# Modulation folds, embedding split, shift products and final normalization reordered in a one-core transformer kernel

## Chip, cores and metric

The kernel runs on 1 core of one Trainium2 chip. The metric is the device time of one execution in microseconds, the median of several runs. The input is one sequence of 512 tokens with 1024 features in float32.

## What is computed

The reference applies three layers to x (512 x 1024). All of it is float32.

```python
# block 1: attention heads beside a short convolution
h = rms_norm(x, pre_norm_gain); q, k, v, z_a, b, c, u, z_c = split(h @ w_in, 8)
attn = rms_norm(diff_attention(q, k, v, lam, slopes), subln_gain) * 0.8 * silu(z_a)   # 4 heads
conv_out = b * causal_conv3(c * u) * silu(z_c)
x = x + rms_norm(concat(attn, conv_out) @ w_out, post_norm_gain)
x = x + sigmoid(x @ w_ple_gate) * rms_norm(p @ w_ple_proj, ple_norm_gain)   # p: embedding, 256 wide
# two modulated layers, i = 0 (Fourier mixer), i = 1 (retention mixer)
sh1, sc1, g1, sh2, sc2, g2 = split(silu(c) @ w_ada[i] + b_ada[i], 6)
x = x + g1 * mixer(rmsnorm(x, g) * (1 + sc1) + sh1)
x = x + g2 * swiglu(rmsnorm(x, g) * (1 + sc2) + sh2)
# end
shf, scf = split(silu(c) @ w_ada_final + b_ada_final, 2)
return rmsnorm(x, final_norm_g) * (1 + scf) + shf
```

The modulation is 14 vectors of 1024 numbers, each the product of one vector of 1024 with a 1024 x 1024 matrix.

## The kernel before

**Layout and the main loop.** Activations lie feature-major, eight slices of 128 features by 512 tokens. Every large product runs in three passes: weights and activations are each split in a high part (float32r) and the rest, and TensorE adds lo x hi, hi x lo and hi x hi in PSUM (`mul`, lines 1708, 1711, 1712; the same for halves of the tokens in lines 1724 to 1728). Weights come as a stream of chunks of 128 x 1024 (eight 128 x 128 tiles) through a ring of four slots: SyncE's queue loads a chunk (line 336), ScalarE writes its high part (`split_w`, line 443), GpSimd writes the rest in four quarters (`lo_part`, line 411), TensorE uses it. TensorE needs 24 matmuls of 512 columns for a chunk. Each engine executes its own written list in order, and semaphores tie the lists together.

**Modulation.** A matrix of the modulation comes as eight chunks of 128 x 1024, loaded by the same SyncE queue between weight chunks (line 342, a ring of two slots; a load waits until the step that used the slot is done). VectorE adds each chunk, times its column of c, to `ada_acc` (one *step*: line 945 for the first of eight, line 948 for the others). The 128 partial sums of each of the 1024 results then have to be added over the partitions. In the four attention heads this is `ada_turn`: TensorE transposes the eight blocks of `ada_acc` into two PSUM banks (line 1895), VectorE adds each along its columns (line 965) and adds the bias (line 967). In the later layers it is `ada_fold` and `ada_rows`: VectorE transposes 32 x 32 blocks (line 972) and adds (line 973), TensorE finishes with four small products (line 1886).

**Attention heads.** A loop over the heads. Inside, TensorE's list holds tiles 4 to 7 of this head with the scores and transposes of the attention between them, and then tiles 8 to 11, the first four of the next head (queries, keys, values, gate). Between them `body_tail` puts, after the n-th product, the weighted values (n = 2), the norm's sum (n = 9) and the modulation's transposes (n = 17). After tile 10 TensorE waits until VectorE has scaled the next head's queries and keys out of PSUM (`evacuate`, line 1208), and computes their first scores (line 1991). VectorE's loop begins with these two evacuations, and ends with the split of the attention's output (line 1285) and `ada_out`. After the last head the projection `out` takes the place of tiles 8 to 11.

**Embedding.** After the heads ScalarE's queue loads the embedding p, ScalarE waits for it and splits it (line 621), VectorE subtracts (line 1296); only then come the weight splits and modulation steps of the projection. The embedding is used by the product after the projection.

**Fourier layer.** `dft1` turns features: four groups g, four token tiles tt each. `rinv_columns` (line 2040) adds the squares for the norm and stands after (g, tt) = (2, 2); ScalarE and VectorE read dft1's tiles with that norm (lines 722, 1381). `shift_columns` (lines 2051, 2052), the products of the shift with the same table, stand after the last tile. `dft2` turns tokens, VectorE combines halves (lines 1410 to 1423) and splits (line 1398), then comes the product `fout`. Modulation steps 41 to 48 stand here: one after group 1, one each in groups 2 and 3, five ahead of the residuals.

**End.** The last normalization works on the front and the back 256 tokens. VectorE computes X x gain x root for each of eight slices (`scaled`, line 1663), ScalarE adds the shift to it (`finish`, line 906; the last two slices on VectorE, line 1680), and the result is stored.

Of the kernel before, what the change touches and what calls it, by code (L numbers as in the profile page):

```python
# [138 lines left out]
def build(nc, W, ADA, XT, PT, COLS, DIST, ROPE, DECAY, OUT):  # L139
# [3 lines left out]
    with ctx:  # L143
# [3 lines left out]
        def sem(name):  # L147
            return ctx.enter_context(nc.semaphore(name))
# [59 lines left out]
        lamt = scr[:, 15 * S:15 * S + 256]  # L208
        MIX, E = area(0, 8), area(8, 8)
# [27 lines left out]
        ada_sum, ada_folded = sem("ada_sum"), sem("ada_folded")  # L237
# [195 lines left out]
        def _(act):  # L433
# [186 lines left out]
            act.wait_ge(p_in, 16)  # L620
            act.activation(b_hi[:, 8:10, :].rearrange("p k s -> p (k s)"), PV, ACT.Copy).then_inc(p_hi, 1)
            c0, t0 = CH["out"], TI["out"]
            for n in range(8):
                if n != 3:
                    split_w(flat, c0 + n + 4)
                if n >= 3:
# [91 lines left out]
            for z in range(2 * NH):  # L718
                wait_tile(act, flat, t1 + z)
                for h in range(2):  # L720
                    half, tt = slice(2 * P * h, 2 * P * (h + 1)), 2 * (z % 2) + h
                    ins = act.activation(a_hi[:, z, half], banks[:, BANK[t1 + z], half], ACT.Identity, bias=zero,
                                         scale=rcol[:, tt:tt + 1])
                ins.then_inc(z_hi, 1)
                if z == 3:
                    act.wait_ge(aux_ready, AUX["fshift"] + 1)
                    split_w(flat, c0 + 4, free=True)
# [176 lines left out]
            def finish(m, scaled, part, done):  # L904
                act.wait_ge(scaled, m + 1)
                act.activation(X[:, m, part], X[:, m, part], ACT.Identity, bias=vector(12)(m)).then_inc(done, 1)
# [18 lines left out]
        def _(dve):  # L925
# [26 lines left out]
            def ada_out(u, g, at=flat, bank=None):  # L952
# [7 lines left out]
                if bank is None:  # L960
                    dve.tensor_tensor(dst, aux[:, 0:KD], b, ALU.add).then_inc(aux_free, 1)
                    return
                for n, half in enumerate((bank, 7)):
                    turned = banks[:, half, :].rearrange("p (f q) -> p f q", q=P)
                    ins = dve.tensor_reduce(ada_col[:, 4 * n:4 * n + 4], turned, AX.X, ALU.add)
                link(ins, at)
                dve.tensor_tensor(dst, ada_col, b, ALU.add).then_inc(aux_free, 1)

            def ada_fold(g, at=flat):
# [4 lines left out]
                                  ALU.add).then_inc(ada_folded, 1)  # L974

# [184 lines left out]
            link(dve.memset(G[:, 0:2], 0.0))  # L1160
            dve.wait_ge(r_ready, 1)
# [55 lines left out]
            with dve.Fori(0, NH) as i:  # L1217
# [70 lines left out]
                ada_out(A0 + 6, 0, at, 4)  # L1288
# [6 lines left out]
            dve.wait_ge(p_hi, 1)  # L1295
            dve.tensor_tensor(b_lo[:, 8:10, :].rearrange("p k s -> p (k s)"), PV,
                              b_hi[:, 8:10, :].rearrange("p k s -> p (k s)").bitcast(fp32),
                              ALU.subtract).then_inc(p_ready, 1)
            t0 = TI["out"]
            for n in range(8):  # L1300
# [5 lines left out]
                ada(k=(1, 1, 1, 1, 1, 2, 1, 0)[n])  # L1306

# [82 lines left out]
            dve.wait_ge(aux_free, AUX["fshift"] + 1)  # L1390
            t0 = TI["dft2"]
# [38 lines left out]
            ada(k=5)  # L1430
# [231 lines left out]
            def scaled(m, part, done):  # L1662
                dve.scalar_tensor_tensor(out=X[:, m, part], in0=X[:, m, part], scalar=gs[:, m:m + 1],
                                         in1=rinv[:, part], op0=ALU.mult, op1=ALU.mult).then_inc(done, 1)
# [5 lines left out]
            scaled(0, FRONT, half_scaled)  # L1670
            scaled(1, FRONT, half_scaled)
            back_tile_made(7, t0, KD - 1, 11)
            for m in range(2, KD):
                scaled(m, FRONT, half_scaled)
            dve.wait_ge(r_ready, 8)
            for m in range(KD):
                scaled(m, BACK, x_scaled)
            dve.wait_ge(x_scaled, KD)
            for m in range(KD - 2, KD):
                dve.tensor_scalar(X[:, m, BACK], X[:, m, BACK], vector(12)(m), None, ALU.add).then_inc(fin, 1)  # L1680
# [3 lines left out]
        def _(pe):  # L1684
# [274 lines left out]
            def body_tail(at, n):  # L1959
# [6 lines left out]
                if n == 17:  # L1966
                    ada_turn(at, A0 + 6, 0, 4)
# [87 lines left out]
            for g in range(NH):  # L2055
                pe.wait_ge(xl, 2 * g + 2)
                for tt in range(TB):
# [330 lines left out]
```

## Time and profile before

| | us |
| --- | --- |
| median of 3 runs | 1554.79 |
| lowest, highest | 1554.63, 1555.78 |
| profiled execution, its own time | 1554.12 |
| its span in the profile | 1552.0 |
| TensorE matmuls, busy | 1537.0 (99%) |
| VectorE, ScalarE, GpSimd busy | 790.5, 597.4, 869.6 |
| last matmul begins | 1542.26 |

The span runs from the first to the last recorded event; the execution's own time is 2.1 us longer. TensorE's matmuls are pipelined: one of 512 columns is shown with 0.39 us, and the next begins 0.23 us after it. So its list is best read by the distance between beginnings, not by the busy share. Times of day below are microseconds from the start of the span.

### The profile page before, as it was taken

What the parts mean: (1) busy time and instruction counts of PE and PEld (TensorE: products, weight loads), DVE (VectorE), ACT (ScalarE), POOL (GpSimd) and SP (SyncE); (2) the same over time, 40 slices, a digit from 0 to 9 for tenths busy, and PEclk for the clock granted to TensorE, in tenths of its full rate; (3) what the DMA queues carried; (4) which work ended last, traced back from release to release, by engine and by line L of the source; (5) the groups of instructions that cost most, each with busy time, mean ns of one, the idle gap of its engine ahead of it and who ended that gap; (6) DMA issues with size and microseconds to landing.
All of it is one profiled execution on the core that took longest, in us unless ns stands there. A gap on an engine that the chain in (4) does not pass through costs nothing.

```text
span 1552.0 us, 21277 instructions
## 1 busy us (share of the span) xinstructions
PE 1537.0 (99%) x7254; PEld 1273.8 (82%) x7254; DVE 790.5 (51%) x1128; ACT 597.4 (38%) x885; POOL 869.6 (56%) x1040
## 2 busy tenths in 40 slices
PE   9999999999999999999999999999999999999997
PEld 7777878887988888888888888888889888888886
DVE  6887776878645543551545424446257454011113
ACT  7444434685522212223444334244345322122223
POOL 6445538647567765775463635535535766555551
PEclk9999999999999999999999999999999999999999
DMA  6534455226265555542232322313212563223321
GB/s 231 191 128 155 164 214 189 82 84 205 95 216 176 202 198 183 192 160 95 89 114 67 109 82 80 97 52 106 95 54 82 201 206 120 98 95 95 95 82 55
DMA packets 58249, 202.97 MB, mean 131 GB/s; under 512 B 6480, under 2 KB 8528, under 8 KB 58192
## 3 DMA queue, kind: packets, MB, share of 16 engines
q1 hardware_dynamic: 56752, 198.74, 37.6%
q10 hardware_dynamic: 1440, 3.44, 0.7%
q8 instruction: 40, 0.66, 0.2%
q14 instruction: 17, 0.14, 0.0%
HBM read 200.05 MB, written 2.10 MB: 130 GB/s over the span
## 4 chain that ended last, share of the span: by engine, by line
PE 76%; POOL 12%; issue 11%; DVE 0%; DMA 0%; ACT 0%; SPq 0%; POOLq 0%; DVEq 0%; ACTq 0%
PE banks L1708 20%; PE banks L1712 20%; PE banks L1711 20%; POOL w_lo L411 12%; PE banks L2212 2%; PE banks L2211 2%; PE banks L2208 2%; PE banks L1724 1%; PE banks L1727 1%; PE banks L1728 1%; PE banks L2248 1%; PE banks L2247 1%; PE banks L2246 1%; PE banks L2235 0%; PE banks L2234 0%
## 5 line engine op out<-in xcount | busy, mean ns | idle before, releaser
L411 POOL TENSOR_TENSOR w_lo<-w_raw,w_hi 128x256 fp32r<-128x256 f32 x1028 | 862.6, 872 | 646.9 <-ACT w_hi L443 646.9
L443 ACT ACTIVATE w_hi<-w_raw 128x1024 fp32r<-128x1024 f32 x257 | 270.1, 1057 | 640.7 <-PE banks L1708 576.0
L1708 PE MATMUL banks<-a_hi,w_lo 128*128 128x512 f32 x1228 | 483.4, 394 | 0.2 <-POOL w_lo L411 0.2
L1712 PE MATMUL banks<-a_hi,w_hi 128*128 128x512 f32 x1228 | 478.2, 389 | 0.0
L1711 PE MATMUL banks<-a_lo,w_hi 128*128 128x512 f32 x1228 | 478.0, 389 | 0.0
L1708 PEld LDWEIGHTS banks<-a_hi,w_lo 128*128 128x128 f32 x1228 | 230.8, 188 | 49.0 <-issue 1.6
L1712 PEld LDWEIGHTS banks<-a_hi,w_hi 128*128 128x128 f32 x1228 | 230.5, 188 | 48.3
L1711 PEld LDWEIGHTS banks<-a_lo,w_hi 128*128 128x128 f32 x1228 | 230.6, 188 | 47.6 <-issue 1.0
L1708 PE MATMUL banks<-b_hi,w_lo 128*128 128x512 f32 x572 | 224.2, 392 | 2.3 <-POOL w_lo L411 2.1
L1712 PE MATMUL banks<-b_hi,w_hi 128*128 128x512 f32 x572 | 222.6, 389 | 0.0
L1711 PE MATMUL banks<-b_lo,w_hi 128*128 128x512 f32 x572 | 222.6, 389 | 0.0
L948 DVE SCALAR_TENSOR_TENSOR ada_acc<-ada_raw,small,ada_acc 128x1024 f32<-128x1024 f32 x98 | 149.5, 1525 | 47.5 <-DMA ada_raw<-in_ADA 45.5
L1105 DVE SCALAR_TENSOR_TENSOR X<-banks,mod,X 128x512 f32<-128x512 f32 x64 | 46.9, 749 | 164.1 <-PE banks L1712 163.9
L1708 PEld LDWEIGHTS banks<-b_hi,w_lo 128*128 128x128 f32 x572 | 107.4, 188 | 26.6 <-issue 3.8
L1711 PEld LDWEIGHTS banks<-b_lo,w_hi 128*128 128x128 f32 x572 | 107.4, 188 | 22.6 <-issue 0.5
L1712 PEld LDWEIGHTS banks<-b_hi,w_hi 128*128 128x128 f32 x572 | 107.3, 188 | 22.4
L1451 DVE TENSOR_TENSOR scr<-scr,banks 128x512 f32<-128x512 f32 x44 | 30.3, 688 | 112.3 <-PE banks L1712 111.9
L1447 DVE SCALAR_TENSOR_TENSOR scr<-scr,banks 128x512 f32<-128x512 f32 x44 | 30.2, 687 | 106.6 <-ACT scr L773 106.6
L1459 DVE SCALAR_TENSOR_TENSOR b_lo<-scr,b_hi 128x512 f32 (+1 forms) x44 | 33.2, 755 | 51.2 <-ACT b_hi L780 51.2
L2208 PE MATMUL banks<-w_lo,a_hi 128*128 128x512 f32 x128 | 49.8, 389 | 0.0
L2211 PE MATMUL banks<-w_hi,a_lo 128*128 128x512 f32 x128 | 49.8, 389 | 0.0
L2212 PE MATMUL banks<-w_hi,a_hi 128*128 128x512 f32 x128 | 49.8, 389 | 0.0
(287 smaller groups left out, 1632.7 us busy)
## 6 DMA issues: line engine op xcount, KB each, us to landing
w_raw<-in_W SPq DMA_DIRECT2D x258, 512.0 KB, 3.5
ada_raw<-in_ADA SPq DMA_DIRECT2D x112, 512.0 KB, 4.3
X<-in_XT SPq DMA_DIRECT2D x8, 256.0 KB, 6.4
scr<-in_DECAY ACTq DMA_DIRECT2D x4, 448.0 KB, 4.0
out<-X SPq DMA_DIRECT2D x2, 512.0 KB, 3.0
w_raw<-in_W SPq DMA_DIRECT2D x2, 256.0 KB, 3.8
scr<-in_PT ACTq DMA_DIRECT2D x1, 512.0 KB, 4.8
scr<-in_ROPE ACTq DMA_DIRECT2D x1, 512.0 KB, 4.6
```

Source lines behind the costliest of these rows:

```text
L411: pool.tensor_tensor(w_lo[:, c % RING, part], w_raw[:, c % RING, part], w_hi[:, c % RING, part].bitcast(fp32), ALU.subtract).then_inc(wlo, 1)
L443: act.activation(w_hi[:, c % RING, :], w_raw[:, c % RING, :], ACT.Copy).then_inc(whi, 1)
L948: ins = dve.scalar_tensor_tensor(out=ada_acc[:, :], in0=src, scalar=cact[:, f:f + 1], in1=ada_acc[:, :], op0=ALU.mult, op1=ALU.add)
L1105: ins = dve.scalar_tensor_tensor(out=X[:, m, :], in0=banks[:, BANK[t], :], scalar=mod[:, KD * g + m:KD * g + m + 1], in1=X[:, m, :], op0=A ...
L1451: read_out(dve.tensor_tensor(HD[:, n, :], SG[:, n, :], banks[:, BANK[u], :], ALU.mult), u)
L1459: dve.scalar_tensor_tensor(out=lo, in0=HD[:, n, :], scalar=0.5, in1=hi.bitcast(fp32), op0=ALU.mult, op1=ALU.subtract).then_inc(hid_ready, 1)
L1708: mm = pe.matmul(out, lo, x_hi, start=first, stop=False)
L1711: pe.matmul(out, hi, x_lo, start=False, stop=False)
L1712: mm = pe.matmul(out, hi, x_hi, start=False, stop=last)
L2208: mm = pe.matmul(out, a_hi[:, k, c], wl, start=(k == 0), stop=False)
L2211: pe.matmul(out, a_lo[:, k, c], wh, start=False, stop=False)
L2212: mm = pe.matmul(out, a_hi[:, k, c], wh, start=False, stop=(k == KD - 1))
```

## The change

Four edits, which share no instruction.

1. **Heads.** `ada_turn` is replaced by `head_ada_fold` on VectorE, ahead of `ada_out`, and `head_ada_rows` on TensorE, after n = 23, the last product of tile 10. Three small additions ahead of the loop make the matrix `head_fold`.
2. **Embedding.** ScalarE's wait and split, and VectorE's subtraction, stand after the third step of the projection's loop.
3. **Fourier.** `rinv_columns` stands one token tile later, `shift_columns` two token tiles earlier, ahead of dft1's last tile. ScalarE then waits for dft1's last tile in its place. Two modulation steps move from the five ahead of the residuals to the end of dft1.
4. **End.** VectorE multiplies X by the root alone, two slices at once; ScalarE applies the gain beside the shift.

```diff
             act.dma_start(PV, PT).then_inc(p_in, 16)
-            act.wait_ge(p_in, 16)
-            act.activation(b_hi[:, 8:10, :]..., PV, ACT.Copy).then_inc(p_hi, 1)
             for n in range(8):
                 if n != 3:
                     split_w(flat, c0 + n + 4)
+                if n == 2:
+                    act.wait_ge(p_in, 16)
+                    act.activation(b_hi[:, 8:10, :]..., PV, ACT.Copy).then_inc(p_hi, 1)
...
                 if z == 3:
-                    act.wait_ge(aux_ready, AUX["fshift"] + 1)
+                    wait_tile(act, flat, t1 + 2 * NH - 1)
                     split_w(flat, c0 + 4, free=True)
...
-            def finish(m, scaled, part, done):
-                act.wait_ge(scaled, m + 1)
-                act.activation(X[:, m, part], X[:, m, part], ACT.Identity, bias=vector(12)(m)).then_inc(done, 1)
+            def finish(m, rooted, part, done):
+                act.wait_ge(rooted, m // 2 + 1)
+                act.activation(X[:, m, part], X[:, m, part], ACT.Identity, bias=vector(12)(m),
+                               scale=gs[:, m:m + 1]).then_inc(done, 1)
...
+            def head_ada_fold(at):
+                dve.wait_ge(ada_sum, at("ada", KD))
+                dve.wait_ge(mix_ready, at("two", 2))
+                link(dve.transpose(head_turned, ada_acc[:, :]), at)
+                ins = dve.tensor_reduce(head_part, head_turned.rearrange("p (j q) -> p j q", q=32), AX.X, ALU.add)
+                ins.then_inc(head_folded, 1)
...
-                ada_out(A0 + 6, 0, at, 4)
+                head_ada_fold(at)
+                ada_out(A0 + 6, 0, at)
...
             dve.wait_ge(aux_free, AUX["fshift"] + 1)
+            ada(k=2)
             t0 = TI["dft2"]
...
             t0 = TI["fout"]
-            ada(k=5)
+            ada(k=3)
...
-            def scaled(m, part, done):
-                dve.scalar_tensor_tensor(out=X[:, m, part], in0=X[:, m, part], scalar=gs[:, m:m + 1],
-                                         in1=rinv[:, part], op0=ALU.mult, op1=ALU.mult).then_inc(done, 1)
+            def rooted(n, part, done):
+                x = X[:, 2 * n:2 * n + 2, part]
+                root = rinv[:, part].unsqueeze(1).broadcast_to([P, 2, HT])
+                dve.tensor_tensor(x, x, root, ALU.mult).then_inc(done, 1)
...
-            def ada_turn(at, u, g, bank):
-                pe.wait_ge(ada_sum, at("ada", KD * (g + 1)))
+            def head_ada_rows(at, u):
+                pe.wait_ge(head_folded, at("one", 1))
                 pe.wait_ge(aux_free, at("aux", u))
-                for f in range(KD):
-                    out = banks[:, bank if f < KD // 2 else 7, f % 4 * P:(f % 4 + 1) * P]
-                    mm = pe.transpose(out, ada_acc[:, f * P:(f + 1) * P], ident)
+                for b in range(4):
+                    mm = pe.matmul(aux[32 * b:32 * b + 32, 0:KD], head_fold, head_part[:, b:32:4], start=True, stop=True)
                 mm.then_inc(aux_ready, 1)
...
-                if n == 17:
-                    ada_turn(at, A0 + 6, 0, 4)
+                if n == 23:
+                    head_ada_rows(at, A0 + 6)
...
-                    if g == 2 and tt == 2:
-                        rinv_columns()
-            shift_columns().then_inc(aux_ready, 1)
+                    if g == 3 and tt == 1:
+                        shift_columns().then_inc(aux_ready, 1)
+                if g == 2:
+                    rinv_columns()
```

TensorE's list at the end of tile 10, in the heads' loop, before (line 1991: the next head's first scores; line 1895, the transposes, stands 18 matmuls further up):

```order
L1708 MATMUL banks<-a_hi,w_lo 128x512
L1711 MATMUL banks<-a_lo,w_hi 128x512
L1712 MATMUL banks<-a_hi,w_hi 128x512
L325 REGISTER_ALU
L1991 MATMUL banks<-scr 128x128 x2
L1697 REGISTER_ALU
L1708 MATMUL banks<-a_hi,w_lo 128x512
```

And now (line 1906: the four small products; lines 1720 to 1724 are `mul`, line 2002 the scores):

```order
L1720 MATMUL banks<-a_hi,w_lo 128x512
L1723 MATMUL banks<-a_lo,w_hi 128x512
L1724 MATMUL banks<-a_hi,w_hi 128x512
L1904 REGISTER_ALU
L1906 MATMUL banks<-scr 32x8 x4
L327 REGISTER_ALU
L2002 MATMUL banks<-scr 128x128 x2
```

Nothing stands between the modulation's product and the scores any more.

VectorE's list at the end of the same loop, before:

```order
L1285 TENSOR_TENSOR b_lo<-tmp,b_hi 128x512
L954 REGISTER_ALU
L965 TENSOR_REDUCE small<-banks 128x4 x2
L932 REGISTER_ALU
L967 ISA
L967 TENSOR_TENSOR mod<-small,cols 128x8
L1217 REGISTER_ALU
L1217 COMPARE_AND_BRANCH
```

And now:

```order
L1293 TENSOR_TENSOR b_lo<-tmp,b_hi 128x512
L977 STREAM_TRANSPOSE tmp<-ada_acc 128x1024
L936 REGISTER_ALU
L978 TENSOR_REDUCE scr<-tmp 128x32
L958 REGISTER_ALU
L964 ISA
L964 TENSOR_TENSOR mod<-banks,cols 128x8
L1225 REGISTER_ALU
L1225 COMPARE_AND_BRANCH
```

The branch leads back to the evacuations of queries and keys. Line 964 (`ada_out`) reads what TensorE's line 1906 writes, and it stands ahead of them.

VectorE's last instructions, before:

```order
L1663 SCALAR_TENSOR_TENSOR X<-X,gs,rinv 128x256 x2
L995 SCALAR_TENSOR_TENSOR X<-banks,mod,X 128x256
L1663 SCALAR_TENSOR_TENSOR X<-X,gs,rinv 128x256 x14
L1680 TENSOR_SCALAR X<-X,mod 128x256 x2
```

And now:

```order
L1676 TENSOR_TENSOR X<-X,rinv 128x2x256
L1000 SCALAR_TENSOR_TENSOR X<-banks,mod,X 128x256
L1676 TENSOR_TENSOR X<-X,rinv 128x2x256 x7
L1691 TENSOR_SCALAR X<-X,gs,mod 128x256 x2
```

Sixteen products of one slice became eight of two.

## Rows read from the trace of the kernel before

**Rows 1.** The page's part 1: busy time, share and instructions

```profile
PE 1537.0 (99%) x7254; PEld 1273.8 (82%) x7254; DVE 790.5 (51%) x1128; ACT 597.4 (38%) x885; POOL 869.6 (56%) x1040
```

**Rows 2.** Timeline, TensorE, first head's end: start, duration, engine, line, operation

```profile
71.21 0.39 PE L1712 MATMUL banks<-a_hi,w_hi 128*128 128x512 f32 x1
71.44 1.03 PE L1895 MATMUL banks<-cols,ada_acc 128*128 128x128 f32 x8
...
72.54 0.40 PE L1711 MATMUL banks<-a_lo,w_hi 128*128 128x512 f32 x1
...
76.18 0.39 PE L1712 MATMUL banks<-a_hi,w_hi 128*128 128x512 f32 x1
76.50 0.49 PE L1991 MATMUL banks<-scr 64*128 64x128 f32 x4
```

**Rows 3.** Timeline, VectorE, the same place

```profile
72.13 0.69 DVE L1285 TENSOR_TENSOR b_lo<-tmp,b_hi 128x512 f32 x1 [0.93 <-ACT b_hi L615]
...
74.19 0.17 DVE L967 TENSOR_TENSOR mod<-small,cols 128x8 f32 x1 [0.17 <-DVE small L965]
74.72 1.29 DVE L1208 TENSOR_TENSOR scr<-banks,scr 128x512 f32<-128x512 f32 x2 [0.37 <-issue]
```

**Rows 4.** Lines 972 and 973 by source: durations in ns, smallest, median, largest

```profile
L972 DVE STREAM_TRANSPOSE scr<-ada_acc x9: 1231/1246/1247, 423.1 to 1295.6; 128x1024 f32<-128x1024 f32 x9
L973 DVE TENSOR_REDUCE cols<-scr x9: 1221/1221/1223, 424.4 to 1296.9; 128x32 f32<-128x1024 f32 x9
```

**Rows 5.** Timeline, TensorE, the first later use of the small products

```profile
432.23 0.39 PE L1712 MATMUL banks<-a_hi,w_hi 128*128 128x512 f32 x1
432.55 0.25 PE L1886 MATMUL banks<-cols 128*32 128x8 f32 x8
...
433.07 0.39 PE L1711 MATMUL banks<-a_lo,w_hi 128*128 128x512 f32 x1
```

**Rows 6.** Timelines, ScalarE and TensorE, after the last head

```profile
233.83 1.06 ACT L621 ACTIVATE b_hi<-scr 128x1024 fp32r<-128x1024 f32 x1 [4.37 <-DMA scr<-in_PT]
...
239.30 0.39 PE L1712 MATMUL banks<-b_hi,w_hi 128*128 128x512 f32 x1
240.42 0.47 PE L1708 MATMUL banks<-b_hi,w_lo 128*128 128x512 f32 x1 [0.73 <-POOL w_lo L411]
```

**Rows 7.** Timelines, Fourier layer: TensorE, VectorE, SyncE's queue, ScalarE, GpSimd

```profile
333.45 0.39 PE L2068 MATMUL banks<-w_lo,b_hi 128*128 128x256 f32 x1 [0.36 <-DVE a_lo L1381]
...
353.34 0.74 DVE L945 TENSOR_SCALAR ada_acc<-ada_raw,small 128x1024 f32<-128x1024 f32 x1
...
355.71 1.27 DVE L948 SCALAR_TENSOR_TENSOR ada_acc<-ada_raw,small,ada_acc 128x1024 f32<-128x1024 f32 x1
...
363.22 1.75 DVE L948 SCALAR_TENSOR_TENSOR ada_acc<-ada_raw,small,ada_acc 128x1024 f32<-128x1024 f32 x1
...
354.11 0.33 SPq L342 DMA_DIRECT2D ada_raw<-in_ADA  x1
...
361.47 1.04 ACT L443 ACTIVATE w_hi<-w_raw 128x1024 fp32r<-128x1024 f32 x1
...
336.78 2.83 POOL L411 TENSOR_TENSOR w_lo<-w_raw,w_hi 128x256 fp32r<-128x256 f32 x4 [3.63 <-ACT w_hi L443]
...
362.59 9.82 POOL L411 TENSOR_TENSOR w_lo<-w_raw,w_hi 128x256 fp32r<-128x256 f32 x9 [1.71 <-ACT w_hi L443]
...
368.07 0.47 PE L1708 MATMUL banks<-b_hi,w_lo 128*128 128x512 f32 x1 [1.33 <-POOL w_lo L411]
```

**Rows 8.** Groups of ScalarE by line and shape: busy us, mean ns

```profile
L843 ACT ACTIVATE b_hi<-scr,small 128x512 fp32r<-128x512 f32 x16 | 11.0, 713 | 0.0
L682 ACT ACTIVATE b_hi<-X,small,gs 128x512 fp32r<-128x512 f32 x8 | 6.4, 802 | 0.0
```

**Rows 9.** Timelines, VectorE and ScalarE, the end

```profile
1541.67 5.62 DVE L1663 SCALAR_TENSOR_TENSOR X<-X,gs,rinv 128x256 f32<-128x256 f32 x14
...
1543.83 4.08 ACT L906 ACTIVATE X<-X,mod 128x256 f32<-128x256 f32 x10
```

More of the change, by code:

```diff
@@ L208, in build @@
         lamt = scr[:, 15 * S:15 * S + 256]
+        head_turned = tmp[:, :, :].rearrange("p a s -> p (a s)")
+        head_fold, head_part = scr[:, 14 * S + 64:14 * S + 96], scr[:, 14 * S + 96:14 * S + 128]
         MIX, E = area(0, 8), area(8, 8)
@@ L236, in build @@
         ada_in = [sem(f"ada_in{s}") for s in range(ADA_RING)]
-        ada_sum, ada_folded = sem("ada_sum"), sem("ada_folded")
+        ada_sum, ada_folded, head_folded = sem("ada_sum"), sem("ada_folded"), sem("head_folded")
         x_in = [sem(f"x_in{m}") for m in range(KD)]
@@ L619, in _ @@
             act.dma_start(PV, PT).then_inc(p_in, 16)
-            act.wait_ge(p_in, 16)
-            act.activation(b_hi[:, 8:10, :].rearrange("p k s -> p (k s)"), PV, ACT.Copy).then_inc(p_hi, 1)
             c0, t0 = CH["out"], TI["out"]
@@ L625, in _ @@
                     split_w(flat, c0 + n + 4)
+                if n == 2:
+                    act.wait_ge(p_in, 16)
+                    act.activation(b_hi[:, 8:10, :].rearrange("p k s -> p (k s)"), PV, ACT.Copy).then_inc(p_hi, 1)
                 if n >= 3:
@@ L950, in ada, with ada_out @@
                     ins.then_inc(ada_sum, 1)
-            def ada_out(u, g, at=flat, bank=None):
+            def ada_out(u, g, at=flat):
                 dve.wait_ge(aux_ready, at("aux", u + 1))
@@ L959, in ada_out @@
                     b = cols[:, bass.ds(at("eight", COL["b_ada"] + KD * g), KD)]
[L960 to L967, printed above, removed]
+                dve.tensor_tensor(dst, aux[:, 0:KD], b, ALU.add).then_inc(aux_free, 1)
             def ada_fold(g, at=flat):
@@ L1160, in _ @@
             link(dve.memset(G[:, 0:2], 0.0))
+            link(dve.tensor_tensor(head_fold, ident[:, 0:32], ident[:, 32:64], ALU.add))
+            for n in (2, 3):
+                link(dve.tensor_tensor(head_fold, head_fold, ident[:, 32 * n:32 * n + 32], ALU.add))
             dve.wait_ge(r_ready, 1)
@@ L1292, in _ @@
             steps[0] = 8 * NH
[L1295 to L1298, printed above, removed]
             t0 = TI["out"]
@@ L1306, in _ @@
                 ada(k=(1, 1, 1, 1, 1, 2, 1, 0)[n])
+                if n == 2:
+                    dve.wait_ge(p_hi, 1)
+                    dve.tensor_tensor(b_lo[:, 8:10, :].rearrange("p k s -> p (k s)"), PV,
+                                      b_hi[:, 8:10, :].rearrange("p k s -> p (k s)").bitcast(fp32),
+                                      ALU.subtract).then_inc(p_ready, 1)
             t1 = TI["ple"]
@@ L1669, in _ @@
                 wait_read(dve, flat, t0 + m)
-            scaled(0, FRONT, half_scaled)
-            scaled(1, FRONT, half_scaled)
+            rooted(0, FRONT, half_scaled)
             back_tile_made(7, t0, KD - 1, 11)
-            for m in range(2, KD):
-                scaled(m, FRONT, half_scaled)
+            for n in range(1, KD // 2):
+                rooted(n, FRONT, half_scaled)
             dve.wait_ge(r_ready, 8)
-            for m in range(KD):
-                scaled(m, BACK, x_scaled)
-            dve.wait_ge(x_scaled, KD)
+            for n in range(KD // 2):
+                rooted(n, BACK, x_scaled)
+            dve.wait_ge(x_scaled, KD // 2)
             for m in range(KD - 2, KD):
-                dve.tensor_scalar(X[:, m, BACK], X[:, m, BACK], vector(12)(m), None, ALU.add).then_inc(fin, 1)
+                dve.tensor_scalar(X[:, m, BACK], X[:, m, BACK], gs[:, m:m + 1], vector(12)(m), ALU.mult,
+                                  ALU.add).then_inc(fin, 1)
         @block.tensor
```

## The prediction, made before the changed kernel was run

> **What bounds the kernel.** I read the page's part 1 first: TensorE is busy 99% of the span, the others about half [rows 1]. That share overstates, since the matmuls are pipelined, so I then read TensorE's timeline by the distance between beginnings. A 512-column matmul begins 0.23 us after the one before (71.21 to 71.44 in [rows 2]), and nearly all of the list runs at that pace. A change can therefore gain only from work taken off TensorE's list, from the few waits in it, or from the end after the last matmul; and any wait added to the list is paid in full. The waits that the edits touch are 0.73 us after the last head [rows 6], 0.36 us ahead of dft1's last tile and 1.33 us in the product fout [rows 7]. The end is carried by VectorE and ScalarE together: 14 products in 5.62 us and 10 additions in 4.08 us, then a store [rows 9]. Anything else that VectorE or ScalarE does matters only where TensorE waits for it.
>
> **Edit 1, the heads.** *Removed from TensorE:* the transposes. The last product before them begins at 71.21, the second matmul after them at 72.54; without them that distance would be two paces, 0.46. They cost 1.33 - 0.46 = 0.87 us per head [rows 2]. *Added:* four small products. The same piece in the later layers takes 432.23 to 433.07 where 0.46 would do, so 0.38 us [rows 5]. Were that all, each head would gain 0.49.
>
> But the products now stand directly ahead of the next head's scores, and VectorE has two evacuations between them. I follow both engines through the first head's end, in the old trace's times.
> - TensorE: without transposes tile 10's last matmul begins at 76.18 - 0.87 = 75.31. The small products begin 0.32 later, as at 432.55 after 432.23 [rows 5]: 75.63.
> - VectorE: line 1285 ends at 72.82 [rows 3]. The block transpose, 1.246 us, needs its buffer and so starts when it has ended, about 72.87; the sum, 1.221 us, follows about 0.04 later [rows 4]. It ends at 75.38, 0.25 before TensorE asks. Tight, but no wait.
> - The small products end at 75.63 + 0.25 = 75.88 [rows 5]. VectorE's `ada_out` starts about 0.07 later, 75.95. From the start of `ada_out` to the end of both evacuations the old trace has 74.19 to 74.72 + 1.29 = 76.01, so 1.82 us, the loop's branch among it [rows 3]. They end at 77.77.
> - The scores can start at about 77.85. They started at 76.50 [rows 2].
>
> So each of the three heads that have a successor is 1.35 us *longer*: TensorE stands about 1.5 us between two pieces 0.25 and 0.49 us long, where before the evacuations were done 0.4 us before it asked. Three times 1.35 is +4.05. After the last head nothing waits for `ada_out`, and the 0.49 is gained: heads **+3.56**. Behind the wait on VectorE are the bias and the next softmax; they come 0.3 later relative to TensorE, whose next need of them is a tile (5 us) away: nothing. The two sums out of PSUM (line 965) go, 2.5 us of transpose and sum come; all of that is in the chain above. The three additions for `head_fold` run on VectorE before the heads' loop, where it waits for the first norm: nothing.
>
> **Edit 2, the embedding.** ScalarE stood 4.37 us for the load and 1.06 us in the split before its weight splits [rows 6], and TensorE paid for it once: 239.30 to 240.42 where 0.23 would do, 0.89 us. Moved behind three splits, the load has long landed, and two chunks go to GpSimd over 4 us sooner. If that cover failed, the most that could be lost is the old 0.89 again. VectorE's 1.2 us subtraction moves ahead of the first reads of the projection's tiles; seven banks let these be late. On SyncE's queue the chunk loads, which wait for GpSimd, and the modulation loads, which wait for steps, both come earlier. **-0.89.**
>
> **Edit 3, Fourier.** The norm's sums come one token tile later, filling a wait there, and so their readers on ScalarE and VectorE come about 0.3 later; the last dft1 tile waits for them [rows 7]. The shift products, about 0.5 us, now run inside that wait instead of after it. Net -0.2, which the next point absorbs. The two early steps fall in a stretch in which VectorE only waits for dft2's edge sums (its next step in [rows 7] is that of 353.34): nothing on VectorE. What they change is SyncE's queue. The load of step 43's chunk goes out at 354.11, after the first step ended (353.34 + 0.74), and every later weight chunk is queued behind it [rows 7]. Now it goes out some 10 us sooner. The wait of 1.33 us at 368.07 hangs on GpSimd's four quarters of fout's fourth chunk: ScalarE splits it at 361.47, GpSimd begins at 362.59 and TensorE goes on at 368.07, 5.4 us for four quarters that took 2.83 at 336.78, with VectorE's step of 1.75 us at 363.22 on top of it [rows 7]. The load of the step after group 3 was there early; now that load (step 46's) is queued behind a weight chunk that waits for GpSimd, goes out at about 361.2 and lands, with the chunk beside it, near 366. So GpSimd gets 363.7 to 366.4 to itself. Against it: the step after group 1 is now an addition to `ada_acc` (1.27) and not the first of eight (0.74, both in [rows 7]), which puts the later groups, the third chunk and ScalarE's split back by 0.4. I take TensorE's resumption at 367.0 instead of 368.07. The bounds are +0.4 (the delay adds, no relief) and -1.5 (wait and restart both gone). **-1.07.** The rule of the Trainium skill, SBUF — State Buffer, section "Who interferes with whom", is that a VectorE instruction with two SBUF inputs and a GpSimd instruction that reads SBUF exclude each other for a whole instruction. These rows show a slowing of 2.6 us beside VectorE's instructions and agree with it in kind. By the rule a step that landed before 366 would put a whole 1.27 us back, and this term would be near zero.
>
> **Edit 4, the end.** VectorE: a pair takes as long as a 128x512 product, 0.60 from start to start (two in 1.29, [rows 3]) instead of 2 x 0.40 (14 in 5.62, [rows 9]). ScalarE: the activation now reads a gain beside the shift. Lines with the one take 713 ns, with both 802 ns [rows 8]: +0.089, over twelve of them on this path. Ten additions in 4.08 begin 0.40 apart, and now 0.49: nine distances and the last one's own length give 9 x 0.1 + 0.09 = +0.98. Ahead of these ten stand four more with the same 0.09, and they wait for pairs, which come 0.14 to 0.2 later than single slices; part of it disappears in the wait for the last slice's square, so I count +0.40 for their start. They end at 1543.83 + 4.08 = 1547.91 before [rows 9], and at about 1549.3 now. VectorE's last two, of 14 products and two additions of about 0.3, ended near 1547.9 too; relieved, it ends near 1547.7 and no longer counts. The last store is issued when both are done, now by ScalarE. **+1.38.** The bounds are -0.7 (ScalarE's gain operand costs nothing in a back-to-back row and VectorE's relief shows) and +1.6.
>
> **Sum:** +3.56 - 0.89 - 1.07 + 1.38 = +2.98 us. The profiled execution took 1554.12 and would take 1557.1; the median of the runs is 0.67 above it, so I forecast **1557.8**. A measurement of this kernel can tell 0.2%, 3.1 us, from no change; the forecast lies just inside.
>
> **Rivals.**
> - *Relief fails (1559.3).* VectorE's fold ends after TensorE asks (only 0.25 us of room, and GpSimd works beside it), 0.2 us more in each of three heads, and the fourth chunk is not relieved (-1.07 becomes 0): 2.98 + 0.6 + 1.07 = +4.6. For it: the thin room, and the page's rule. Against: the fold's rows vary by under 20 ns.
> - *The round trip is partly hidden (1555.6).* If the wake-ups and the branch cost less than I count, a head is 0.6 longer, not 1.35: 2.98 - 2.2 = +0.8. Against: only fixed delays of rows are in the chain.
> - *Faster (1550.2).* The other side, in one mechanism: TensorE does not wait for the evacuations, because VectorE gets past `ada_out` before tile 10 ends. Then every head gains 0.49: -1.96 in place of +3.56. With fout's wait fully gone (-1.5) and the end at its lower bound (-0.7) that is about -5, 1549.7; with the other terms as forecast 1552.3. It decides at 76.4 us: the evacuations must end before TensorE's scores could start. In VectorE's list they stand behind a wait for the very product that follows tile 10, so I see little room.
> - *The end costs nothing (1556.4).* Both engines share the end; if the gain operand is free, +1.38 becomes 0.
>
> **How the numbers follow.** Forecast 0.55, split evenly by the 0.2% bound because it lies on it (0.27 slower, 0.28 same); relief fails 0.20, slower; partly hidden 0.13 and end free 0.05, same; faster 0.07. That is faster 0.07, same 0.46, slower 0.47. The range takes in the first four cases with their bounds: 1554.6 to 1559.8.
>
> **What would show it.** In the changed profile: scores (now line 2002) starting about 1.9 us after the small products, with VectorE's evacuations ended just before, three times; the distance from head to head 1.35 us longer; no wait at the projection's second half; the fourth fout chunk's wait under 0.5 us; line 909 at about 0.58 us each and ten of them in 5 us; the last store issued 1.4 us later behind the last matmul. A head shorter than before would make the prediction wrong at its root.

## The result, and the profile after

The changed kernel takes 1561.69 us (median of 6 runs, 1558.71 to 1562.65), the one before 1555.04 in 6 runs beside it (1554.63 to 1557.02). The ratio is 1.0035, with a 95% interval of 1.0024 to 1.0045. So it is slower, as forecast, but by 6.65 us between the medians and not by 3, and the time is above the range of 1554.6 to 1559.8. The means of the same runs lie 5.6 us apart, nearer to the ratio: two of the six runs were near 1559. The profiled execution took 1561.93, with a span of 1559.9 instead of 1552.0.

The page's part 1 of the changed kernel, which answers to [rows 1]:

```profile
PE 1538.0 (99%) x7254; PEld 1273.4 (82%) x7254; DVE 800.3 (51%) x1123; ACT 598.4 (38%) x885; POOL 864.7 (55%) x1040
```

TensorE has as many instructions as before and its busy time has risen by 1.0 us; the share says nothing. What tells is the start of the same TensorE instruction in both traces:

| place on TensorE | before | after | difference |
|---|---|---|---|
| first scores of head 1 | 27.58 | 27.97 | +0.39 |
| scores of head 2 | 76.50 | 79.32 | +2.82 |
| scores of head 3 | 129.06 | 134.99 | +5.93 |
| scores of head 4 | 181.62 | 190.58 | +8.96 |
| start of the first dft1 tile, past the last head and the embedding | 320.27 | 327.72 | +7.45 |
| product fout, third chunk | 361.02 | 368.77 | +7.75 |
| product fout, fourth chunk | 368.07 | 374.85 | +6.78 |
| statistics products after the last matmul of the model | 1541.07 | 1548.23 | +7.16 |
| span | 1552.0 | 1559.9 | +7.9 |

The heads cost 2.4, 3.1 and 3.0 us, and I had forecast 1.35 each. The windows view shows part of the reason. For each stretch it gives the length, the busy time of each engine with its instructions, then PEclk, TensorE's granted clock. First the changed kernel, from the scores of head 2 to those of head 3 and on to those of head 4, then the kernel before, the first of these stretches:

```profile
79.30:135.00 55.70, 53.57 (x246) 41.76 (x246) 43.17 (x70) 22.25 (x40) 26.32 (x33) 0.97 0.42 151
135.00:190.60 55.60, 53.49 (x246) 41.70 (x246) 42.38 (x70) 22.13 (x40) 25.84 (x33) 0.97 0.41 151
```

```profile
76.50:129.06 52.56, 52.56 (x246) 41.23 (x245) 41.88 (x70) 22.13 (x40) 26.20 (x34) 1.00 0.43 160
```

As many matmuls as before, 246, are busy 1 us longer, with 2.1 us idle beside them, and the granted clock is 0.97 where it was 1.00. The loss of clock is not spread out. The same view of two short stretches, just behind the first and the second end of a head, has a granted clock of 0.50:

```profile
81.00:84.00 3.00, 3.00 (x9) 2.33 (x8) 2.54 (x6) 1.23 (x5) 3.00 (x5) 0.50 0.20 76
136.00:138.50 2.50, 2.50 (x7) 1.95 (x6) 1.61 (x6) 1.83 (x5) 1.81 (x4) 0.50 0.29 116
```

TensorE's timeline of the changed kernel at the first and the second end of a head:

```profile
75.79 0.39 PE L1724 MATMUL banks<-a_hi,w_hi 128*128 128x512 f32 x1
76.93 0.25 PE L1906 MATMUL banks<-scr 128*32 128x8 f32 x8 [0.75 <-DVE scr L978]
79.32 0.49 PE L2002 MATMUL banks<-scr 64*128 64x128 f32 x4 [2.14 <-DVE scr L1216]
79.74 0.50 PE L1720 MATMUL banks<-a_hi,w_lo 128*128 128x512 f32 x1
...
80.56 0.51 PE L1720 MATMUL banks<-a_hi,w_lo 128*128 128x512 f32 x1
80.87 0.63 PE L1723 MATMUL banks<-a_lo,w_hi 128*128 128x512 f32 x1
81.29 0.63 PE L1724 MATMUL banks<-a_hi,w_hi 128*128 128x512 f32 x1
...
84.20 0.39 PE L1720 MATMUL banks<-a_hi,w_lo 128*128 128x512 f32 x1
...
132.63 0.25 PE L1906 MATMUL banks<-scr 128*32 128x8 f32 x8
134.99 0.55 PE L2002 MATMUL banks<-scr 64*128 64x128 f32 x4 [2.11 <-DVE scr L1216]
135.47 0.79 PE L1720 MATMUL banks<-a_hi,w_lo 128*128 128x512 f32 x1
136.06 0.63 PE L1723 MATMUL banks<-a_lo,w_hi 128*128 128x512 f32 x1
...
139.82 0.40 PE L1720 MATMUL banks<-a_hi,w_lo 128*128 128x512 f32 x1
```

The small products (line 1906) and the wait for VectorE's evacuations (line 1216) stand where the prediction put them. What it did not have is behind them: from 80.87 to 83.85, and from 136.06 to 138.62, a 512-column product begins 0.43 us after the one before it instead of 0.23 (one distance on each side is mixed). With the granted clock of 0.50 beside it, that is the 1.2 GHz level instead of the 2.4 GHz one. At the third end of a head there is the same wait and no such stretch; the granted clock is 1.00 there from 191 to 194:

```profile
190.58 0.49 PE L2002 MATMUL banks<-scr 64*128 64x128 f32 x4 [2.11 <-DVE scr L1216]
191.00 0.50 PE L1720 MATMUL banks<-a_hi,w_lo 128*128 128x512 f32 x1
...
193.86 0.39 PE L1720 MATMUL banks<-a_hi,w_lo 128*128 128x512 f32 x1
```

This one is the yardstick for the cost. Twelve distances from the first product behind the scores are 2.86 us here (191.00 to 193.86), 4.46 after the first wait (79.74 to 84.20) and 4.35 after the second (135.47 to 139.82): 1.60 and 1.49 us lost, and 0.06 more in the second's scores. Together 3.15 us. The number of such stretches seems to differ from run to run: the mean granted clock over a whole run is 0.994 in the slowest of the six (1562.65) and 0.997 in the fastest (1558.71), and 0.995 in the profiled one with its two.

VectorE at the first end of a head, the counterpart of [rows 3] and [rows 4]:

```profile
69.89 1.28 DVE L952 SCALAR_TENSOR_TENSOR ada_acc<-ada_raw,small,ada_acc 128x1024 f32<-128x1024 f32 x1 [1.57 <-DMA ada_raw<-in_ADA]
...
73.50 0.69 DVE L1293 TENSOR_TENSOR b_lo<-tmp,b_hi 128x512 f32 x1 [0.93 <-ACT b_hi L617]
74.30 1.25 DVE L977 STREAM_TRANSPOSE tmp<-ada_acc 128x1024 f32<-128x1024 f32 x1
75.58 1.22 DVE L978 TENSOR_REDUCE scr<-tmp 128x32 f32<-128x1024 f32 x1
77.37 0.17 DVE L964 TENSOR_TENSOR mod<-banks,cols 128x8 f32 x1 [0.57 <-PE banks L1906]
77.89 1.29 DVE L1216 TENSOR_TENSOR scr<-banks,scr 128x512 f32<-128x512 f32 x2 [0.35 <-issue]
```

The chain is the one that I followed, but it runs 1.4 us late in this head (line 1293 starts at 73.50, line 1285 at 72.13 before), because the modulation step ahead of it waits for its load until 69.89. So the fold ends after TensorE asks, and TensorE waits 0.75 us ahead of the small products too. In the second head it does not.

### The profile page after: what moved, and what is told of

The parts are those of the page before. It is cut to its first block, busy times and chain, and to the rows that moved or that the text cites. A ratio compares the mean times of both kernels' runs of the same rounds, so it can differ in the third digit from the quotient of the medians.

```text
span 1559.9 us, 21274 instructions
## 1 busy us (share of the span) xinstructions
PE 1538.0 (99%) x7254; PEld 1273.4 (82%) x7254; DVE 800.3 (51%) x1123; ACT 598.4 (38%) x885; POOL 864.7 (55%) x1040
## 4 chain that ended last, share of the span: by engine, by line
PE 75%; POOL 12%; issue 11%; ACT 1%; DMA 0%; SPq 0%; POOLq 0%; DVE 0%; ACTq 0%
PE banks L1720 20%; PE banks L1723 20%; PE banks L1724 20%; POOL w_lo L413 12%; PE banks L2220 2%; PE banks L2224 2%; PE banks L2223 2%; PE banks L1736 1%; PE banks L1739 1%; PE banks L1740 1%; PE banks L2258 1%; PE banks L2260 1%; PE banks L2259 1%; PE banks L2245 0%; PE banks L2247 0%
## 5 line engine op out<-in xcount | busy, mean ns | idle before, releaser
L952 DVE SCALAR_TENSOR_TENSOR ada_acc<-ada_raw,small,ada_acc 128x1024 f32<-128x1024 f32 x98 | 156.0, 1592 | 43.0 <-DMA ada_raw<-in_ADA 40.5
```

The source lines that it names most:

```text
L952: ins = dve.scalar_tensor_tensor(out=ada_acc[:, :], in0=src, scalar=cact[:, f:f + 1], in1=ada_acc[:, :], op0=ALU.mult, op1=ALU.add)
```

## The experiments

Four explanations stood against each other for what was missing. **A**: the heads' new waits, and the slow clock behind them. **B**: the excess comes from the other edits. **C**: the slow stretches have nothing to do with TensorE's idle time. **D**: the fold is simply too long for VectorE, whatever the order. Each kernel was timed beside runs of the kernel before on the same chip: median 1554.81 of 27 runs for the first four, 1555.0 of 33 for the last four. "Offset" below is the start of a TensorE instruction less the start of the same one before. It compares two single executions, and these differ where nothing was changed too: at the start of dft1 the three kernels further down whose edits all act later have offsets of +0.48, +0.71 and +1.66, part of them from the start of the first head, part from the wait that stands at 240.42 before. So differences of a few tenths in one offset prove little by themselves.

### The heads' edit alone

Edit: the kernel before, with only these parts of the change: `head_fold`, `head_ada_fold`, `ada_out` without the sums out of PSUM, `head_ada_rows` behind tile 10.

> Only the heads edit on the kernel before. Theory A (waits and clock): the three round trips cost about 1.35 us each and TensorE then runs at half pace for some 3.5 us after most of them, so the whole excess sits here: about +7 to +8 us against before (1562 to 1563), with matmul distances of 0.43 us behind the scores in at least one head. Theory B (my forecast's chain was right and the excess comes from the other edits): +3.6 us, 1558.6, and no slow stretch.

Measured: 1561.27 us (1560.77 to 1562.92, 5 runs), ratio 1.0046, interval 1.0033 to 1.006. The scores have offsets of +1.62, +4.73 and +7.81, and from the first dft1 tile to the last matmul the offset is +7.36 everywhere. The time lies a little under the 1562 to 1563 expected. The mean granted clock of its runs is 0.995 to 0.997, and 0.997 to 0.999 in the 27 of the kernel before. TensorE's timeline at the first end of a head, with the small products in line 1901:

```profile
75.73 0.25 PE L1901 MATMUL banks<-scr 128*32 128x8 f32 x8
78.12 0.49 PE L1997 MATMUL banks<-scr 64*128 64x128 f32 x4 [2.15 <-DVE scr L1214]
...
80.35 0.63 PE L1715 MATMUL banks<-a_hi,w_lo 128*128 128x512 f32 x1
80.78 0.63 PE L1718 MATMUL banks<-a_lo,w_hi 128*128 128x512 f32 x1
```

What follows: the whole loss sits in this edit, and B falls. Here nothing delays the first fold, and the head's end comes out close to the hand-made chain: small products at 75.73 (forecast 75.63), scores at 78.12 (forecast 77.85). The last head, which nothing waits for, gives 0.45 back (+7.81 to +7.36; 0.49 was forecast). The slow stretch is there again after the first two waits and again not after the third.

### All edits but the heads'

Edit: the change without the parts of the experiment above.

> The embedding, Fourier and end edits without the heads edit. Theory A: -0.9 for the embedding, about -0.3 for Fourier, +0.7 for the end, together -0.4 us (1554.6), granted clock as before. Theory B: +3 us or more (1558).

Measured: 1553.47 us (1552.77 to 1554.1, 11 runs), ratio 0.9992, interval 0.9983 to 1.0001. Offsets: +0.56 before the embedding, -0.43 behind it; -0.47 at the first dft1 tile and -1.26 at the last matmul; the span is 0.5 shorter. So the embedding gives 0.99 (forecast 0.89), Fourier 0.79 (forecast 1.07), and the end costs about 0.7 (forecast 1.38). The three work as forecast in sign and are together near no change (the interval just takes in 1; the time is 1.1 us under the expected 1554.6).

### TensorE's idle time filled

Edit, on the changed kernel. The seven products write a bank whose contents nobody reads before they are overwritten, and the output doesn't change:

```diff
                     if n == 10:
+                        for _ in range(7):
+                            pe.matmul(banks[:, 4, :], ones_r[:, :], a_hi[:, 0, :], start=True, stop=True)
                         for q in (8, 9):
```

> The changed kernel with seven matmuls of 512 columns, written to a free bank, between the small products and the next head's scores, so TensorE works through the wait without the wait being shorter. Theory A: the scores start at the same distance behind tile 10 (within 0.2 us), no slow stretch follows, and the time falls by about 3 us (1558.5). Theory C (the slow stretches have nothing to do with the idle time before them): they stay, and the time stays at 1561.7 or above.

Measured: 1557.93 us (1557.11 to 1558.82, 11 runs), ratio 1.0018, interval 1.0009 to 1.0027. By the medians that is 3.8 us faster than the changed kernel (3.0 by the means), with more work in it. TensorE's timeline:

```profile
75.96 0.25 PE L1906 MATMUL banks<-scr 128*32 128x8 f32 x8 [0.23 <-DVE scr L978]
76.14 1.90 PE L1999 MATMUL banks<-a_hi,ones_r 128*128 128x512 f32 x7
78.35 0.49 PE L2004 MATMUL banks<-scr 64*128 64x128 f32 x4 [0.31 <-DVE scr L1216]
...
81.65 0.39 PE L1720 MATMUL banks<-a_hi,w_lo 128*128 128x512 f32 x1
81.88 0.39 PE L1723 MATMUL banks<-a_lo,w_hi 128*128 128x512 f32 x1
```

The windows view of all the heads' ends in one stretch, with a granted clock of 1.00:

```profile
70.00:250.00 180.00, 178.56 (x836) 139.36 (x835) 140.19 (x220) 73.63 (x129) 89.47 (x111) 1.00 0.47 165
```

The scores begin 2.39 us after the small products, just as in the changed kernel, so the delay by VectorE is untouched. But no stretch at 0.43 follows, in any of the heads, and the scores' offsets are +1.85, +3.50 and +4.99: about 1.6 a head. None of the eleven runs has a mean granted clock under 0.997. C falls: the slow stretches go with the idle time, and they are the largest part of what the prediction lacked. Not all of the gain is theirs: at the scores of head 4 this kernel is 3.97 us ahead of the changed one, the stretches were 3.15 of that, and about 0.5 is a shorter wait for the first fold (0.23 instead of 0.75). That the median then falls on my forecast of 1557.8 is partly luck, since smaller errors of both signs remain.

### The evacuations ahead of the addition

Edit, on the changed kernel: VectorE does the next head's two evacuations after the fold and before it waits for the small products.

```diff
-            with dve.Fori(0, NH) as i:
+            def one_head(i, more):
...
-                evacuate(at, 0, Q, RPRE)
-                evacuate(at, 1, K, RPRE)
...
                 head_ada_fold(at)
+                if more:
+                    evacuate(at, 8, Q, RPRE)
+                    evacuate(at, 9, K, RPRE)
                 ada_out(A0 + 6, 0, at)
+            evacuate(flat, 0, Q, RPRE)
+            evacuate(flat, 1, K, RPRE)
+            with dve.Fori(0, NH - 1) as i:
+                one_head(i, True)
...
+            one_head(NH - 1, False)
```

> The changed kernel with the next head's two evacuations on VectorE ahead of ada_out (behind the fold), so that they no longer wait for the small products. Theory A: TensorE waits about 0.8 us per head in place of 2.4, scores come 0.25 us later than in the kernel before, no slow stretch: about 1555 us. Rival D (VectorE's fold itself is too long for the head, whatever the order): still 1559 or more, the wait only moves.

Measured: 1554.83 us (1553.32 to 1558.59, 11 runs), ratio 1.0002, interval 0.9993 to 1.0011: the time before. TensorE's timeline, first and second end of a head:

```profile
77.10 0.25 PE L1914 MATMUL banks<-scr 128*32 128x8 f32 x8 [0.70 <-DVE scr L978]
78.31 0.49 PE L2010 MATMUL banks<-scr 64*128 64x128 f32 x4 [0.96 <-DVE scr L1216]
...
130.16 0.25 PE L1914 MATMUL banks<-scr 128*32 128x8 f32 x8
131.37 0.49 PE L2010 MATMUL banks<-scr 64*128 64x128 f32 x4 [0.96 <-DVE scr L1216]
```

The round trip between the engines is gone; what stays is the length of the evacuations behind the fold. In this trace a wait of 0.96 is followed by no slow stretch: the granted clock is 1.00 from 70 to 250. That isn't shown for every execution: the slowest of the eleven runs, 1558.59, has a mean granted clock of 0.995 where the others have 0.997 or 0.998, and no trace of it was kept. D falls as well: this is the changed kernel but for the place of two instructions (and the last head written out behind the loop), and the order alone is worth about 6.9 us by the medians, 6.0 by the means.

### The early modulation steps alone, and the shift products alone

Edits: the kernel before with one thing each. Steps: `ada(k=2)` ahead of the edge sums and `ada(k=3)` in place of `ada(k=5)` behind them. Products: the norm's sums one tile later, and the shift columns inside dft1's last tile.

> Only the two modulation steps moved to the end of dft1, on the kernel before. If SyncE's queue order is what counts: third fout chunk 0.4 to 0.5 us later (a longer step after group 1), fourth chunk's wait shortened so that TensorE is 0.4 to 0.5 us ahead of the kernel before at the end of fout: 1554.3. Rival (the two early steps do nothing, the gain came from the moved products): no offset at the end of fout.

> Only rinv_columns and shift_columns moved, on the kernel before. My step says -0.2 us at the start of dft2, -0.3 as the runs so far show, and that this is lost again at fout's fourth chunk, which hangs on VectorE's and ScalarE's chain: 0 to -0.3 us at the end of fout. Rival: the whole Fourier gain is here, -0.8 us.

Measured: steps 1554.74 us (1554.07 to 1555.64, 10 runs), ratio 0.9997, interval 0.9988 to 1.0006; products 1554.48 (1554.15 to 1555.31, 10 runs), ratio 0.9995, interval 0.9985 to 1.0004. By their times neither differs from no change. By offsets, the steps lose 0.46 at fout's third chunk and win 0.97 at the fourth, net -0.5; the products win 0.3 at dft2 and keep 0.25 of it. Their sum is near the 0.79 of the second experiment. Both halves of the fout term have the forecast sign, the delay of the third chunk (forecast 0.4) and the relief of the fourth (resumption 1.07 earlier was forecast, net of the delay; 0.5 came).

### The end alone

Edit: the kernel before with the new last norm (pairs times the root on VectorE, the gain beside the shift on ScalarE). The stores are as before.

> Only the end: VectorE multiplies pairs by the root, ScalarE applies gain and shift. If the gain operand costs ScalarE 0.09 us an instruction: ten of them in 5.0 instead of 4.1 us, ScalarE's last 1.3 us later, span +0.7 us (1555.5). Rival (VectorE's relief shows): -0.7 us, 1554.1.

Measured: 1555.79 us (1555.19 to 1557.0, 11 runs), ratio 1.0003, interval 0.9994 to 1.0012: +0.8 by the medians. ScalarE's and its queue's timeline:

```profile
1545.84 5.01 ACT L906 ACTIVATE X<-X,mod,gs 128x256 f32<-128x256 f32 x10
...
1551.28 0.49 ACTq L922 DMA_DIRECT2D out<-X  x1
```

The ten additions take 5.01 (4.08 before, forecast about 5.06), but the last issue of a store takes 0.49 where it took 0.70. The term is about +0.7 to +0.8. The time itself doesn't differ from no change.

### The version that beats both

Edit: the heads' edit with the two evacuations placed earlier still, where VectorE stands waiting for ScalarE's split (behind the third operation of the head's norm, ahead of `b_lo`), with the embedding and Fourier edits, and with the old end.

```diff
                                          op0=ALU.mult, op1=ALU.mult).then_inc(o_out, 1)
+                if more:
+                    evacuate(at, 8, Q, RPRE)
+                    evacuate(at, 9, K, RPRE)
...
                 head_ada_fold(at)
                 ada_out(A0 + 6, 0, at)
```

> The heads edit with the two evacuations of the next head before line 1285's counterpart, in VectorE's wait for ScalarE, embedding and Fourier edits as in the change, the old end. If the heads edit loses only by its place: no TensorE wait over 0.3 us around the small products, each head 0.3 to 0.5 us shorter than in the kernel before, and about -3.3 us in all (1551.5). Rival (the fold's extra 1.2 us of VectorE work is paid somewhere in the head anyway): 1553.5 or more, as in the run without the heads edit.

Measured: 1551.98 us (1550.53 to 1552.92, 11 runs), ratio 0.9978, interval 0.9969 to 0.9987, faster than both kernels. TensorE's timeline and VectorE's at the first end of a head (line 1912 the small products, 2008 the scores):

```profile
76.86 0.25 PE L1912 MATMUL banks<-scr 128*32 128x8 f32 x8 [0.17 <-DVE scr L977]
77.09 0.49 PE L2008 MATMUL banks<-scr 64*128 64x128 f32 x4
```

```profile
72.24 1.28 DVE L1215 TENSOR_TENSOR scr<-banks,scr 128x512 f32<-128x512 f32 x2
73.44 0.68 DVE L1293 TENSOR_TENSOR b_lo<-tmp,b_hi 128x512 f32 x1
```

The evacuations fill a wait that stood there (0.93 in [rows 3]), `b_lo` comes no later than in the changed kernel, and the scores follow the small products after 0.23 instead of 2.39. The heads are now a gain: the scores' offsets are +0.59, -0.11 and -0.11, then the last head, the embedding and Fourier bring -2.38 at the last matmul. The forecast's 0.49 a head did not come in each: in the first and the third TensorE still waits, 0.17 and 0.54, for the fold. The expectation that no wait over 0.3 would be left there missed by the second of these.

## Why the prediction was wrong

**The direction and the mechanism were right.** The rival "Faster" was rightly small: TensorE does wait for the evacuations in all three heads, because VectorE has them behind the wait for the small products. Each wait has the size of the chain: 2.35 to 2.39 us from the small products to the scores, 2.22 forecast. Of the rival "Relief fails" one half came: VectorE's fold ended after TensorE asked, but 0.82 us too late in one head, not 0.2 in each of three. (Its sum gives 1559.4 and not the 1559.3 at its head, and "Faster" is headed 1550.2 where its two sums give 1549.7 and 1552.3; neither moves the forecast.)

**The term that was mis-sized is edit 1's, "three times 1.35".** I charged a wait by its length and took the matmuls behind it at their full pace; 1.6 and 1.5 us of slow clock stood behind two of the three. Measured against the profiled executions, the forecast was +2.98 and 7.81 came, 4.83 more:

| part | us | from |
|---|---|---|
| 1.2 GHz stretches behind two of three waits | +3.15 | the twelve distances above |
| the first fold ends late, TensorE waits for it | +0.91 | 0.82 between 75.79 and 76.93, and 0.09 |
| the chain of each head longer than counted | +0.44 | 2.39, 2.36 and 2.35 against 2.22 |
| start of the first head | +0.39 | offset at 27.97 |
| last head and embedding better than counted | -0.13 | 1.51 against 1.38 |
| Fourier: in this execution -0.29, not -1.07 | +0.78 | +7.45 to +7.16 |
| end: +0.74, not +1.38 | -0.64 | span less last matmul |

They add up to 4.90; the span rose 0.1 us more than the execution's own time.

The first line alone takes the time out of my range. That it comes from TensorE's idle time is shown by the filled wait, which took every slow stretch away and left the delay between small products and scores as it was; the traces with shorter waits agree. The second and the fourth differ from execution to execution: in the other four kernels with this fold the wait for it in head 1 was 0, 0.23, 0.70 and 0.17 (in the order of the experiments), and the offset at the first scores is +0.03 with the heads' edit alone and +0.39 with the others alone. They were not taken apart further. The waits in [rows 6] and [rows 7], 0.73 and 1.33, gave no warning: no slow stretch is behind them. But that also means that no row of before priced a wait of 2 us, and I took its length as its price, without a bound above.

**Edit 2** held: 0.99 measured, 0.89 forecast. The wait that it removes is 0.73 in the trace of the kernel before, and 0.76 to 1.39 in the four experiments that keep it.

**Edit 3** held in its two halves but not in its size. The fourth chunk's wait is 0.36 instead of 1.33, under the 0.5 that I named, and the third chunk comes 0.5 to 0.6 later than the second does. From GpSimd's first quarter of that chunk to TensorE it is 4.52 us (370.33 to 374.85) with one VectorE step beside it, and was 5.48 with two (362.59 to 368.07): that is the relief. In the changed kernel a new wait took half of the gain back: the offset is +6.80 at 390.60, +7.09 at 391.57 and +7.16 at the last matmul. TensorE, VectorE and GpSimd there:

```profile
368.77 0.47 PE L1720 MATMUL banks<-b_hi,w_lo 128*128 128x512 f32 x1 [0.70 <-POOL w_lo L413]
374.85 0.47 PE L1720 MATMUL banks<-b_hi,w_lo 128*128 128x512 f32 x1 [0.36 <-POOL w_lo L413]
...
391.57 0.36 PE L1736 MATMUL banks<-b_hi,w_lo 128*128 128x256 f32 x1
...
379.86 8.04 DVE L952 SCALAR_TENSOR_TENSOR ada_acc<-ada_raw,small,ada_acc 128x1024 f32<-128x1024 f32 x1 [4.07 <-DMA ada_raw<-in_ADA]
...
388.70 2.07 DVE L1110 SCALAR_TENSOR_TENSOR X<-banks,mod,X 128x512 f32<-128x512 f32 x3
...
370.33 16.49 POOL L413 TENSOR_TENSOR w_lo<-w_raw,w_hi 128x256 fp32r<-128x256 f32 x20 [1.71 <-ACT w_hi L445]
```

One VectorE step shows 8.04 us here, where the median of the 98 steps in this trace is 1.57. It ends 1.08 after GpSimd's unbroken row of 20 quarters (370.33 + 16.49 = 386.82); the residuals behind it start at 388.70, and TensorE is held for their banks. But the overlap alone doesn't make a step long. The two steps before it lie in the same row of quarters and took 1.75 and 1.37. And the five experiments that contain the moved steps have the same step beside a row of 20 quarters as well, where it took 1.29 to 1.78; in the kernel with the evacuations ahead of the addition:

```profile
372.94 1.78 DVE L952 SCALAR_TENSOR_TENSOR ada_acc<-ada_raw,small,ada_acc 128x1024 f32<-128x1024 f32 x1 [4.07 <-DMA ada_raw<-in_ADA]
...
363.42 17.47 POOL L413 TENSOR_TENSOR w_lo<-w_raw,w_hi 128x256 fp32r<-128x256 f32 x20 [1.71 <-ACT w_hi L445]
```

So the 8.04, and the 0.36 us of TensorE behind it, belong to this one execution, and their cause is open. What the rows do show is a price per step: the 20 quarters take 16.49 us with two ordinary steps beside them (the changed kernel), 17.47 to 17.56 with three (the five experiments) and 19.49 with five (the kernel before), so about 1 us of GpSimd for each, and not the 1.27 that the prediction took from the rule. The rule of the Trainium skill, SBUF — State Buffer, section "Who interferes with whom", is that such instructions of the two engines lock each other out for a whole instruction. The price per step agrees with it; a hold of 8 us is more than one instruction of GpSimd, and no run isolates it.

**Edit 4** was half right. ScalarE's gain operand costs what [rows 8] said, ten additions in 5.01:

```profile
1551.35 5.01 ACT L909 ACTIVATE X<-X,mod,gs 128x256 f32<-128x256 f32 x10
...
1556.80 0.49 ACTq L925 DMA_DIRECT2D out<-X  x1
```

And the last issue before:

```profile
1548.33 0.70 ACTq L921 DMA_DIRECT2D out<-X  x1
```

The additions end 1.29 later than in [rows 9], counted from the statistics products at 1541.07 and 1548.23. But the last issue took 0.49 instead of 0.70, and from its end to the end of the span it is 2.6 (1557.29 to 1559.9) where it was 3.0 (1549.03 to 1552.0). The prediction has the last store issued "now by ScalarE"; it was ScalarE's before too, and no store changed its engine. What changed is its neighbour: before, SyncE's last store was issued at the same time (1548.32, 0.67 us), and in the changed kernel at 1556.35, 0.44 ahead. In the ten traces the last issue of ScalarE took 0.70 to 0.72 with the old end (five of them) and 0.48 to 0.49 with the new one (the other five). I had the end's work and left out its stores.

## What to carry to other kernels

On a TensorE that otherwise never stops, charge a new wait of about 2 us with more than its length: here 1.5 to 1.6 us came on top in two of three cases, and which two could not be told ahead. Before a result from another engine is needed, look at what that engine has queued behind its own wait for TensorE: two evacuations moved ahead of one small addition, into a wait that was there anyway, and the end left as it was, turned 6.7 us slower into 3 us faster. And when a stall can't be avoided, see whether the cheaper repair is to move the work, not to fill the gap: filling gave back 3.8 us, moving 6.9 (by the medians).

## What the runs showed of the hardware that was not expected

- The granted clock fell after waits of 2.1 to 2.15 us in a stream that was dense before and after: 4 times in 6 (the changed kernel and the heads' edit alone, each after heads 1 and 2 and not after head 3). The fall came at once (135.47) or after more than 1 us of full pace (from 79.32 to 80.56 in the rows above). In the profiled execution, waits of 0.70 and 0.96, one right behind the other (the evacuations ahead of the addition, head 1), had none behind them. Why the third never shows it was not settled. The Trainium skill, TensorE: Matmul & The Clock Gate, section "A second HAM failure mode: psum-queue depth-cycling", says that frequent short idle times between groups of matmuls can make the clock oscillate. The runs agree in that a short idle time went ahead of each fall; here it was one wait in some 50 us and not a frequent one.
- Seven matmuls of no use made a kernel 3.8 us faster (1557.93 against 1561.69).
- One VectorE step lasted 8.04 us beside an unbroken row of GpSimd instructions, once among the 98 steps of each of ten traces; no other was over 1.94. Ordinarily each step beside such a row lengthened the row by about 1 us.
- Two stores issued at the same time by ScalarE and SyncE took 0.70 and 0.67 us to issue; with 0.44 us between their starts ScalarE's took 0.49.
